# Routing of the expert stage: router products between output products, a norm factor per token, the first pair's rows by a product

## The reference

```python
x = x + merged @ w_out[l]
h2 = _rmsnorm(x, g_ffn[l])          # x * rsqrt(mean(x*x) + EPS) * g
pg = softmax(h2 @ w_rg + b_rg)      # 4 groups, the best one is taken
el = h2 @ w_re + b_re               # 32 experts
pe_top, e_idx = top_k(softmax(el of the group), 2)
weights = pg_top * pe_top / sum(pe_top)
x = x + sum over the two: weight * ((silu(h2 @ w_gate[e]) * (h2 @ w_up[e])) @ w_down[e])
```

## Time and profile before

| | us |
|---|---|
| median of 3 runs | 3894.08 |
| lowest, highest | 3888.68, 3894.92 |
| the profiled execution itself | 3894.22 |
| its span, first to last instruction | 3892.4 |
| last output product taken up | 3169.45 |
| first pair's gate product starts | 3248.33 |
| mean granted TensorE clock | 0.919 |

### The profile page before, as it was taken

The page is one execution under the profiler, slowest core; times in us unless marked ns, Lnnn a source line. Parts: engine busy times, 40 slices in busy tenths (PEclk is TensorE's granted clock), DMA queues, the critical chain, the costliest instruction groups (busy, mean ns, idle before and its releaser), DMA issues.

```text
span 3892.4 us, 39687 instructions
## 1 busy us (share of the span) xinstructions
PE 3422.6 (88%) x16652; PEld 2352.5 (60%) x16652; DVE 1117.3 (29%) x1836; ACT 1068.5 (27%) x1818; POOL 709.3 (18%) x344
## 2 busy tenths in 40 slices
PE   7998899979758898888889999988899986989896
PEld 5675688856447777756568876455685562333332
DVE  5342310142763433353231122275131220000001
ACT  3542433334331211213243332134321121111111
POOL 3021344422200000002134441000241121000000
PEclk9999999988877977889999999999999988999998
DMA  3231244311100000022122323210122237989996
GB/s 112 87 108 44 87 162 134 99 58 52 49 0 2 1 1 1 12 87 81 44 82 92 98 87 99 76 33 1 49 77 79 81 119 303 387 327 372 375 375 279
DMA packets 217759, 448.62 MB, mean 115 GB/s; under 512 B 14192, under 2 KB 191376, under 8 KB 204656
## 3 DMA queue, kind: packets, MB, share of 16 engines
q1 hardware_dynamic: 200832, 400.58, 28.4%
q10 hardware_dynamic: 6720, 25.17, 1.6%
q0 software_dynamic: 10032, 20.35, 1.5%
HBM read 502.67 MB, written 31.46 MB: 137 GB/s over the span
## 4 chain that ended last, share of the span: by engine, by line
PE 77%; DMA 8%; DVE 7%; ACT 4%; issue 3%; POOL 1%; SPq 0%; ACTq 0%; POOLq 0%; DVEq 0%
PE product_banks L560 12%; PE product_banks L561 12%; PE product_banks L562 12%; PE product_banks L532 8%; PE product_banks L1859 5%; PE product_banks L1892 3%; DMA A<-in_w_up 3%; DMA Wr<-expert_rows 3%; PE product_banks L624 3%; PE product_banks L2323 2%; PE product_banks L2313 1%; PE product_banks L2315 1%; PE product_banks L1122 1%; PE score_banks L1103 1%; PE product_banks L1339 1%
## 5 line engine op out<-in xcount | busy, mean ns | idle before, releaser
L469 POOL TENSOR_TENSOR Wr_parts<-Wr,Wr_parts 128x1024 fp32r<-128x1024 f32 x186 | 447.2, 2406 | 1429.8 <-ACT Wr_parts L446 1429.8
L561 PE MATMUL product_banks<-A_parts,Wr_parts 128*128 128x512 f32 x1408 | 559.1, 397 | 0.0
L446 ACT ACTIVATE Wr_parts<-Wr 128x1024 fp32r<-128x1024 f32 x186 | 196.0, 1058 | 729.9 <-PE product_banks L562 636.1
L1859 PE MATMUL product_banks<-A,Wr 128*64 128x512 f32 x1504 | 338.9, 598 | 15.7 <-DMA A<-in_w_up 13.3
L560 PE MATMUL product_banks<-H_parts,Wr_parts 128*128 128x512 f32 x728 | 297.2, 408 | 24.4 <-POOL Wr_parts L469 20.8
L561 PEld LDWEIGHTS product_banks<-A_parts,Wr_parts 128*128 128x128 f32 x1408 | 269.6, 191 | 62.0 <-issue 2.2
L560 PE MATMUL product_banks<-A_parts,Wr_parts 128*128 128x512 f32 x680 | 269.8, 397 | 31.1 <-DVE A_parts L482 15.6
L562 PE MATMUL product_banks<-H_parts,Wr_parts 128*128 128x512 f32 x728 | 290.9, 400 | 0.0
L469 POOL TENSOR_TENSOR shared_con_parts<-Wr,shared_con_parts 128x1024 fp32r<-128x1024 f32 x80 | 193.1, 2414 | 446.5 <-ACT shared_con_parts L446 446.5
L562 PE MATMUL product_banks<-A_parts,Wr_parts 128*128 128x512 f32 x680 | 267.8, 394 | 0.0
L1859 PEld LDWEIGHTS product_banks<-A,Wr 128*64 128x64 f32 x1504 | 112.4, 138 | 237.4 <-issue 234.4
(11 more groups left out here) (430 smaller groups left out, 5459.0 us busy)
## 6 DMA issues: line engine op xcount, KB each, us to landing
A<-in_w_gate SPq DMA_DIRECT2D x32, 2048.0 KB
A<-in_w_up SPq DMA_DIRECT2D x32, 2048.0 KB
A<-in_w_down SPq DMA_DIRECT2D x32, 2048.0 KB
Wr<-in_m_w_up SPq DMA_DIRECT2D x32, 1024.0 KB, 5.3
Wr<-in_m_w_down SPq DMA_DIRECT2D x32, 1024.0 KB, 4.9
Wr<-in_w_in SPq DMA_DIRECT2D x32, 1024.0 KB, 5.6
Wr<-in_c_w_kv SPq DMA_DIRECT2D x16, 1024.0 KB, 5.2
expert_rows<-LB ACTq DMA_DIRECT2D x12, 1024.0 KB, 4.2
```

What stands on the lines that cost most here:

```text
L446: nc.scalar.activation(weight_parts(s)[0], loaded_part(s), ACT.Copy).then_inc(*mark("weights_high", s))
L469: nc.gpsimd.tensor_tensor(lo, loaded_part(s), hi, ALU.subtract).then_inc(*mark("weights_split", s))
L561: pe.matmul(bank[:, :], hi[:, k, :], x_lo, start=False, stop=False)
L1859: mm = pe.matmul(BK[r, 0 if kind == "gate" else 1, :], XT[b % 2][:, k * P + CAP * h:k * P + CAP * h + CAP], unit_rows((kind, b, h))[:, k, ...
```

## The change

Router products, squares and their sums are moved between the output products. ScalarE writes the tiles with their gain only and squares them after each output tile; VectorE adds the squares; TensorE makes the router products of tile t - 1 after output tile t. After the last tile TensorE sums the squares per token into one column each, ScalarE takes the root of 128x4 numbers, and VectorE applies its reciprocal to the router products while it adds the bias. The normed rows get the factor when ScalarE copies them out. The ranks are counted before the residual rows are turned, the weights of the two choices are computed after "extras_known", a root's table is loaded before the output products, and router weights and constants are loaded earlier. The first pair's rows are no longer read back from memory (they are still scattered): VectorE compares 128 place numbers with the destination rows (zeros and ones), and TensorE multiplies HR by them. Router sums, squares' sums and ranks lie in the two banks S2 instead of product banks.

```diff
+        ("D", "beyond", 32), ("D", "row", 1), ("D", "place", 128),
...
+    put("place", i[None].repeat(P, 0))
...
@@ -1463,8 +1466,10 @@
                         *mark("products_read_by_act", (f"gate{b}", j)))
             for j in range(8):
                 high_part(act, ("merged", j), high(j), tile(42 + j), [("merged", j)])
+            nc.scalar.activation(small[:, 252:253], eps_col(1.0), ACT.Sqrt)
             for j in range(8):
                 take_product(act, "wout2", j)
+                gained_act(act, j)
 
...
-            product(pe, "wout2", parts(0, 8), low_ready("merged"))
+            pe.wait_ge(*at("loaded_router0", 0))
+            pe.wait_ge(*at("loaded_router1", 0))
+            product(pe, "wout2", parts(0, 8), low_ready("merged"),
+                    then=lambda t: t and router_pe(pe, t - 1))
...
+                if j >= 2:
+                    row_squares_dve(dve, j - 1)
...
+        RSC = small[:, 240:244]
+        DSUMS = [lbf[:, 1000:1004], lbf[:, 1004 + NX:1008 + NX]]
+        FIRST = SQ[:, 0, :].rearrange("p (m r) -> p m r", m=TT)
+
+        def square_of_row(t):
+            return LW if t == 0 else SQ[:, 1, :] if t == DT - 1 else (B6, B7)[t % 2][:, :]
+
+        def gained_act(act, t):
+            act.wait_ge(*at("products_read_by_dve", ("wout2", t)))
+            nc.scalar.activation(hn(t), X[:, t, :], ACT.Copy, scale=pc("g_ffn", t)).then_inc(
+                *mark("gained_ready", t))
+            if 3 <= t < DT - 1:
+                act.wait_ge(*at("squares_added", ("h2", t - 2)))
+            nc.scalar.activation(square_of_row(t), X[:, t, :], ACT.Square).then_inc(
+                *mark("squares_ready", ("h2", t)))
+
+        def row_squares_dve(dve, t):
+            dve.wait_ge(*at("squares_ready", ("h2", t)))
+            if t > 1:
+                dve.wait_ge(*at("squares_added", ("h2", t - 1)))
+            nc.vector.tensor_tensor(LW, square_of_row(t), LW, ALU.add).then_inc(
+                *mark("squares_added", ("h2", t)))
+
+        def router_pe(pe, k):
+            pe.wait_ge(*at("gained_ready", k))
+            for m in range(TT):
+                mm = pe.matmul(S2[:, 0, 36 * m:36 * m + 36], hn(k)[:, m * P:(m + 1) * P],
+                               RT[:, k, :], start=(k == 0 and m == 0), stop=(k == 7),
+                               skip_group_check=True)
+            if k == 7:
+                mm.then_inc(*mark("router_done", 0))
+
+        def row_sums_pe(pe, part, last):
+            for m in range(TT):
+                mm = pe.matmul(S2[:, 1, 256 + m:257 + m], part[:, m * P:(m + 1) * P], ones[:, 0:1],
+                               start=(m == 0 and not last), stop=last, skip_group_check=True)
+            return mm
...
         def route_dve(dve):
-            norm_apply(dve, "h2", xt, hn, lambda t: pc("g_ffn", t))
...
             dve.wait_ge(*at("router_done", 0))
-            link(dve, nc.vector.tensor_tensor(
-                LG, BK[:, 0, 0:144].rearrange("p (m n) -> p m n", m=4),
-                BR[:, None, :].broadcast_to([P, 4, 36]), ALU.add))
+            dve.wait_ge(*at("row_root_ready", 0))
+            nc.vector.reciprocal(RSC, RSC).then_inc(*mark("row_scale_ready", 0))
+            dve.wait_ge(*at("row_scale_ready", 0))
+            for m in range(TT):
+                ins = nc.vector.scalar_tensor_tensor(
+                    out=LG[:, m, :], in0=S2[:, 0, 36 * m:36 * m + 36], scalar=RSC[:, m:m + 1],
+                    in1=BR, op0=ALU.mult, op1=ALU.add)
+            link(dve, ins)
...
-            dve.wait_ge(*at("margin_exp_ready", 0))
...
+                link(dve, nc.vector.tensor_reduce(DSUMS[k], oe[k], AX_X, ALU.add))
+                link(dve, nc.vector.tensor_copy(rows_of[:, 4 * k:4 * k + 4], DSUMS[k]))
...
+
+            for m in range(TT):
+                ins = nc.vector.tensor_scalar(FIRST[:, m, :], cc("place"), DSUMS[0][:, m:m + 1], None,
+                                              ALU.is_equal)
+            link(dve, ins)
+            for m in range(TT):
+                ins = nc.vector.scalar_tensor_tensor(
+                    out=FIRST[:, m, :], in0=cc("place"), scalar=DSUMS[1][:, m:m + 1],
+                    in1=FIRST[:, m, :], op0=ALU.is_equal, op1=ALU.add)
+            ins.then_inc(*mark("first_places_ready", 0))
...
+            dve.wait_ge(*at("margin_exp_ready", 0))
+            link(dve, nc.vector.tensor_reduce(SMG, EXG, AX_X, ALU.add))
...
+        def route_act(act):
+            act.wait_ge(*at("row_squares_summed", 0))
+            nc.scalar.activation(RSC, S2[:, 1, 256:260], ACT.Sqrt, scale=1.0 / D,
+                                 bias=eps_col(EPS)).then_inc(*mark("row_root_ready", 0))
+
+            def rows(key, dst, **kw):
+                for m in range(TT):
+                    for g in range(2):
+                        act.wait_ge(*at("turned", (key, m, g)))
+                        nc.scalar.activation(dst[:, m, g * 512:(g + 1) * 512],
+                                             (B6, B7)[g][:, :], ACT.Copy,
+                                             **{n: v(m) for n, v in kw.items()}).then_inc(
+                            *mark("rows_ready", (key, m, g)))
+
+            act.wait_ge(*at("row_scale_ready", 0))
+            rows("h2", HR, scale=lambda m: RSC[:, m:m + 1])
             act.wait_ge(*at("group_shifted", 0))
             nc.scalar.activation(EXG, SHG, ACT.Exp).then_inc(*mark("group_exp_ready", 0))
             act.wait_ge(*at("margin_ready", 0))
             nc.scalar.activation(EX, DM, ACT.Exp).then_inc(*mark("margin_exp_ready", 0))
...
+            rows("xr", XR)
...
         def route_pe(pe):
-            norm_sum(pe, "h2")
...
+            pe.wait_ge(*at("squares_added", ("h2", DT - 2)))
+            row_sums_pe(pe, LW, False)
+            router_pe(pe, DT - 1)
+            pe.wait_ge(*at("squares_ready", ("h2", DT - 1)))
+            row_sums_pe(pe, SQ[:, 1, :], True).then_inc(*mark("row_squares_summed", 0))
+            turn_rows_pe(pe, hn, "h2", lambda m, g: [("rows_ready", ("h2", m - 1, g))] if m else [])
             pe.wait_ge(*at("choices_ready", 0))
             for m in range(TT):
...
+                    pe.matmul(S2[:, 1, 32 * m:32 * m + 32], ones if k < m else cc("tri"),
...
             mm.then_inc(*mark("ranks_done", 0))
+            turn_rows_pe(pe, xt, "xr", lambda m, g: [("rows_ready", ("xr", m - 1, g) if m else
+                                                      ("h2", 3, g))])
+
+        def first_rows_pe(pe):
+            pe.wait_ge(*at("first_places_ready", 0))
+            pe.wait_ge(*at("rows_ready", ("xr", TT - 1, 1)))
+            for k in range(8):
+                for m in range(TT):
+                    mm = pe.matmul((B6, B7)[k // 4][:, (k % 4) * P:(k % 4 + 1) * P],
+                                   HR[:, m, k:D:DT], FIRST[:, m, :], start=(m == 0),
+                                   stop=(m == TT - 1))
+            mm.then_inc(*mark("pair_rows_turned", 0))
...
             for j in range(8):
                 sp.wait_ge(*at(f"scattered{j}", 0))
-            sp.wait_ge(*at("rows_ready", ("h2", 3, 1)))
-            load_rows(sp, 0)
             load_rows(sp, 1)
...
         def experts_pe(pe):
-            pair_turn_pe(pe, 0)
+            first_rows_pe(pe)
...
+            for j in range(8) if b == 0 else ():
+                act.wait_ge(*at(f"scattered{j}", 0))
...
-                for n in ("cx", "cc", "cb", "gate0", "gate1", "gate2", "wout2"):
-                    split_weights(pool, n)
-
-            if "D" in phases:
-                if "C" in phases:
-                    pool.wait_ge(*at("products_read_by_dve", ("wout2", 7)))
-                pool.dma_start(shared[:, 0:CWIDTH["D"]], a.conD).then_inc(
-                    *mark("loaded_conD", 0, 16))
...
+                for n in ("cx", "cc", "cb", "gate0", "gate1", "gate2", "wout2"):
+                    split_weights(pool, n)
+
+            if "D" in phases:
+                third_uses = [s for s in range(len(split_uses)) if parts_slot[s] == 2]
+                pool.wait_ge(*at("products_done", split_uses[third_uses[-1]]))
+                pool.dma_start(shared[:, 0:CWIDTH["D"]], a.conD).then_inc(
+                    *mark("loaded_conD", 0, 16))
                 scatter_pool(pool)
                 extras_pool(pool)
```

62 lines of the change are left out of this document (15 added, 47 removed).

## The result

The changed kernel took 3855.32 us in the median of 4 runs (3853.82 to 3855.83), the kernel before 3891.38 us in 4 runs beside it (3885.87 to 3894.92): a ratio of 0.9906, 95% interval 0.9884 to 0.9928. Five later runs gave 3860.82 us (3857.32 to 3862.62) against 3891.13 us, 0.9939 (0.9916 to 0.9962). So it is some 30 to 36 us faster; forecast were 3856.0 us. The profiled execution has a span of 3851.9 us.

A forecast was written before the change was run, and what follows sets the result against it. A chain of latencies between last output product and first expert product, then weights through the DMA, was taken as the bound; third pair's up weights 38.2 us earlier, carried to the end from 3894.2, gave 3856.0 us, range 3849 to 3867.

The forecast's parts named there:

- output products grow by: Output products: 1.5 us for the early square root's table load plus 5.4 us for six router groups, 6.9 us in all.
- T to logits: From the last residual addition (T) to the logits: sums, last router products, root, reciprocal and scaled additions, 6.25 us.
- T to known rows: From the last residual addition (T) through choices and ranks to known destination rows: 20.85 us, rows known 25.7 us earlier.
- first rows' product: TensorE's 32 products of 128 columns that make the first pair's rows: 7.2 us at full clock, twice that at low.
- first gate product: First pair's gate product: 13.95 us instead of 15.94, 2 us saved because TensorE is busy before it.
- wait before third pair's up: TensorE ready at 3254.5 waits for third pair's up weights, there at 3262.0: 7.5 us.
- T to third pair's up: From the last residual addition (T) to the third pair's up product: 85.65 us, that product 38.2 us earlier than before.
- (1): Third pair's up: TensorE decides, not the weights, needing 476 GB/s from the DMA; time 3851.5 us, chance 0.12.
- (2): Clock stays at 1.2 GHz from the tail on; rows known 4.9 us later, gain 30.7 us, 3863.5 us; chance 0.20.
- (3): First pair's product still waits for what passes through memory; only 25.7 us won, 3868.5 us; chance 0.04.
- (4): Clock drops inside the output products because small-column runs stand between them; costs 43.5 us, 3899.5 us; chance 0.03.
- (5): Six later expert cycles find a worse rhythm, 9.9 us a cycle, 59 us; 3915 us, chance 0.03.

## Why the prediction was right

Step by step, forecast against the first profile of the changed kernel:

| step | forecast | measured |
|---|---|---|
| output products grow by | 6.9 | 6.2 |
| T to logits | 6.25 | 5.56 |
| choices to ranks read | 3.3 | 3.4 |
| T to known rows | 20.85 | 20.2 |
| places | 1.8 | 2.0 |
| first rows' product | 7.2 | 15.5 |
| T to gate product | 31.25 | 38.9 |
| first gate product | 13.95 | 15.65 |
| wait before third pair's up | 7.5 | 2.72 |
| T to third pair's up | 85.65 | 90.2 |
| third pair's up to end | 592.3 | 589.2 |

- **Output products:** the sum is right within 0.7 us, one of its two terms is not. Residual additions are 6.38 us apart instead of 5.44, 0.94 for each router group against 0.90. The growth of 6.2 us is 409.9 less 403.7. The six router groups make 5.6 us of it (409.95 - 404.35) against 5.4 forecast, the table load 0.6 us against 1.5: with the load and without the groups the stretch is 404.35 us, 0.6 above the 403.74 of before. The load does hold up the first output product by the 1.5 us, but that product would have started at the low clock, which the sum left out: starting later, it takes some 0.7 us less. The drain of about 1.38 us that the Trainium skill ("ScalarE: Activation LUTs", "What ACT_TABLE_LOAD costs") puts beside each switch is absent here: the load starts 0.02 us behind the end of the work before it, and the activation behind it 1.29 us later.
- **Tail, ranks, rows:** right within 0.7 us each; sums and router groups ran at full clock up to 3177, so the 0.9 us that I had added for a falling clock were not needed. The order of ranks was worth its 9.5 us (forecast 9.3).
- **First rows' product:** the mis-sized term. I took the spacing of 0.112 us from products that load neighbouring columns; no row of before showed a load of every eighth column in front of a 128-column product. With neighbouring columns it took 7.4 us. I had named 14 us as a sign of error, and that sign came.
- **Gate product:** 15.65 us, because the clock fell to 0.50 near 3211.7, 0.4 us into it, although TensorE had been at full clock through the product before; the gap between is 1.2 us.
- **Weights:** the mechanism was right (without the extra expert's bytes the wait is gone), the wait too large, since TensorE came 7.7 + 1.7 us later. The weights came later too: 70.0 us behind the known rows (3192.69 to 3262.67), forecast 64.8 (3197.2 to 3262.0). The windows (columns as in the earlier trace rows) show the place:

```profile
3192.70:3204.70 12.00, 10.52 (x47) 10.28 (x47) 4.39 (x17) 1.09 (x2) 8.98 (x10) 1.00 0.79 323
3204.70:3213.90 9.20, 8.03 (x32) 6.23 (x33) 0.00 (x0) 2.37 (x3) 1.88 (x2) 0.88 0.96 356
3213.90:3222.00 8.10, 8.10 (x36) 2.54 (x34) 0.00 (x0) 0.60 (x1) 1.00 (x1) 0.92 0.65 249
3222.00:3262.50 40.50, 35.59 (x172) 12.88 (x168) 1.39 (x2) 4.94 (x9) 1.99 (x2) 1.00 0.97 397
```

I read the 249 GB/s of 8.1 us as the ring waiting for the gate product to free a slot, so that the longer product held the weights up too. The sum of bytes, 12 x 0.323 + 9.2 x 0.356 + 8.1 x 0.249 + 40.5 x 0.397 = 25.2 MB, is the forecast one (25.3). With neighbouring columns the up product stood 64.6 us behind the known rows (3195.21 to 3259.78) and at T + 85.4: both as forecast, and so they support that reading.
- **The end:** the error of 4.6 us at the third pair was balanced by 3.1 us in the later cycles, 0.7 us in the output products and 3.1 us in untouched code ahead of them. So the closeness of 3855.3 to 3856.0 is partly luck. The later median of 3860.8 is no better test: in its profile the untouched code took 6.2 us more than before (GpSimd's first low part at 2771.89 instead of 2765.72).
- **Rivals:** (1) is out: a wait for weights was there, and with the shorter product two up products waited (1.71 and 2.01 us). (2) did not come as priced: the clock fell to 0.50 near 3177.6, just as the logits came, and rose again at 3181 in the turns of rows (the windows at 3177, 3178 and 3181 stand below), and the rows were known at T + 20.2, with none of the 4.9 us. Its tail did come in the two kernels with the early table. (3) is out for the changed kernel; the kernel that reads the first pair through memory has the third pair's up at T + 97.0, 11.6 us behind that of the kernel with neighbouring columns (T + 85.4), where 12.5 was its price over the forecast. (4) is out: router groups at 0.97 us, clock 1.00. (5) is out: the six cycles from the third pair's up took 75.2 to 78.0 us, before 75.3 to 78.6.

```profile
3177.00:3178.00 1.00, 0.57 (x6) 0.33 (x4) 0.89 (x5) 0.72 (x2) 0.00 (x0) 0.80 0.00 0
3178.00:3179.00 1.00, 0.98 (x5) 0.98 (x6) 0.83 (x6) 0.55 (x1) 0.00 (x0) 0.50 0.00 0
...
3181.00:3182.00 1.00, 0.72 (x7) 0.48 (x6) 0.86 (x6) 0.93 (x2) 0.00 (x0) 0.99 0.00 0
```

All TensorE work in these windows is transposes. The Trainium skill, "TensorE: Matmul & The Clock Gate", Part 4 (PE-mode transpose), states that they don't engage the full clock; the row at 3181 speaks against it, as the one at 3208 did before.

## What to carry to other kernels

When a product is priced from the trace, take a row with the same spacing of columns in the loaded operand, not only the same shape. Where work that the matrix engine does beside a chain of small steps is moved between its large products, it runs at their clock; gathered in the tail, the same products ran in part at half of it and cost up to double (1.9 us against 0.97 for eight instructions). Count changes from a common instruction behind the untouched code, and judge gains of a few microseconds by that count over several profiles, of either kernel on the same chip. When an engine starts late, look first at the semaphore update that it waited for: that tells whether the engine or its signal was late.

## What the runs showed of the hardware

- A float32 weight load of 128x128 took 192 ns with neighbouring columns, 196 ns with every second, 329 ns with every fourth and 335 ns with every eighth, and a product of 128 columns behind it 0.117 or 0.24 us per instruction (3.74 against 7.70 to 7.77 us for 32). That a step of 2 is still nearly free I had not expected.
- While eight scatters were under way, TensorE's semaphore update came 2.4 to 6.6 us behind the modelled end of its product in six profiles on one chip, and 0.01 to 0.02 us behind it in three on another and one on a third; ScalarE's copy started 0.02 to 0.03 us behind the update in all of them with ScalarE's copy. The same program was late on one chip and in time on the other.
- The clock fell to 0.50 near 3211.7, 0.4 us into the first gate product (a mean of 0.87 in the window at 3211 and 0.50 at 3212), though TensorE had been busy at full clock for the 15.5 us before but for a gap of 1.2 us. Behind the 7.4 us product and the same gap it stayed at full clock (13.95 us).
- The clock's fall behind the last residual addition repeated by program: T + 5.0 to T + 5.2 in nine profiles, T + 2.3 in both with the early table, T + 3.8 in both with the router products behind.
